# Attention with alternating local and full heads, and turned outputs in the local scores' bank

## What is computed

```python
# A: 8 local heads (2 key heads), a window of 128 keys to each side, a bias by distance, a sink per head
s = einsum(q, k_window) * scale + bias;  s = where(valid, s, -1e30)
m = max(max(s), sink);  e = exp(s - m);  p = e / (sum(e) + exp(sink - m));  oa = p @ v_window
# B: 8 full heads (2 key heads), over all T keys
p = softmax(einsum(q, k) * scale);  ob = p @ v
mixed = concat([rmsnorm(oa, g_out_a), rmsnorm(ob, g_out_b)])
```

## Time and profile before

| | us |
|---|---|
| median of 3 runs | 1623.55 (1623.14 to 1625.81) |
| the profiled execution | 1623.36 |
| its span | 1621.5 |
| TensorE busy | 1447.0 (89%) |
| VectorE busy | 932.7 (58%) |
| ScalarE busy | 721.8 (45%) |
| GpSimd busy | 182.2 (11%) |
| mean granted TensorE clock | 0.947 |

### The profile page before, as it was taken

How to read it: one execution, slowest core, us unless ns; L and a number is a source line. 1 busy time by engine, 2 the same in 40 slices (tenths; PEclk the granted TensorE clock), 3 DMA queues, 4 the chain that set the end, 5 groups by cost and what they waited for, 6 DMA issues and landing times. The chain is left out here.

```text
span 1621.5 us, 21520 instructions
## 1 busy us (share of the span) xinstructions
PE 1447.0 (89%) x7320; PEld 1016.2 (63%) x7320; DVE 932.7 (58%) x1324; ACT 721.8 (45%) x1157; POOL 182.2 (11%) x255
## 2 busy tenths in 40 slices
PE   5999997599999969869998969999999999948997
PEld 4777775365565535458887746666666666627885
DVE  5444443377677748723347856677676676643553
ACT  4333433376666747722221544444444444423332
POOL 1111111000000000010000111112112121021110
PEclk9999998699999979989998979999999999978999
DMA  8533322713111054064432756878878788753331
GB/s 257 94 111 110 110 97 85 252 64 114 70 63 55 20 190 156 29 208 156 140 123 87 262 169 220 263 252 270 256 261 267 254 262 265 245 164 126 126 135 65
DMA packets 118847, 261.53 MB, mean 161 GB/s; under 512 B 7648, under 2 KB 37472, under 8 KB 115720
## 3 DMA queue, kind: packets, MB, share of 16 engines
q1 hardware_dynamic: 110592, 233.55, 41.2%
q0 software_dynamic: 7168, 25.17, 6.7%
q10 hardware_dynamic: 1032, 2.10, 1.1%
HBM read 194.20 MB, written 66.58 MB: 161 GB/s over the span
## 5 line engine op out<-in xcount | busy, mean ns | idle before, releaser
L1742 DVE TENSOR_TENSOR moe_w_lo<-ring,moe_w_hi 128x2048 fp32r<-128x2048 f32 x96 | 220.3, 2296 | 163.5 <-ACT moe_w_hi L1681 163.4
L1681 ACT ACTIVATE moe_w_hi<-ring 128x2048 fp32r<-128x2048 f32 x96 | 183.7, 1914 | 204.0 <-PE moe_p_g L1864 82.2
L1413 PE MATMUL mix_p_big<-kept_out_w,mix_m_hi 128*128 128x512 f32 x384 | 126.4, 411 | 4.6 <-DVE mix_m_lo L1288 2.4
L510 PE MATMUL proj_p_out<-proj_w_hi,proj_h_hi 128*128 128x512 f32 x264 | 110.8, 420 | 9.5 <-DVE proj_q_hl L408 9.5
L1872 PE MATMUL moe_p_gu<-ring,moe_xT_r 128*64 128x512 f32 x512 | 116.9, 598 | 0.0
L510 PE MATMUL proj_p_out<-proj_w_lo,proj_h_hi 128*128 128x512 f32 x264 | 105.0, 398 | 0.0
L510 PE MATMUL proj_p_out<-proj_w_hi,proj_h_lo 128*128 128x512 f32 x264 | 104.9, 397 | 0.0
L962 DVE TENSOR_REDUCE sample_ntop<-sample_p_s 128x1 f32<-128x1024 f32 x64 | 78.2, 1222 | 37.4 <-PE sample_p_s L784 36.7
L798 PEld LDWEIGHTS sample_p_t<-sample_ident_r,sample_probs_r 128*128 128x128 f32 x688 | 73.1, 142 | 23.2 <-ACT sample_probs L900 6.6
L1413 PEld LDWEIGHTS mix_p_big<-kept_out_w,mix_m_hi 128*128 128x128 f32 x384 | 73.1, 196 | 21.4 <-issue 2.6
L798 PE MATMUL sample_p_t<-sample_ident_r,sample_probs_r 128*128 128x128 f32 x688 | 80.1, 246 | 5.0 <-ACT sample_probs L900 2.5
(11 more groups left out here) (298 smaller groups left out, 3122.4 us busy)
## 6 DMA issues: line engine op xcount, KB each, us to landing
ring<-in_w_gate SPq DMA_DIRECT2D x32, 1024.0 KB, 5.6
ring<-in_w_up SPq DMA_DIRECT2D x32, 1024.0 KB, 7.6
ring<-in_w_down SPq DMA_DIRECT2D x32, 1024.0 KB, 7.2
qT_d<-proj_qT SPq DMA_DIRECT2D x12, 1024.0 KB, 3.9
sample_q<-qT_d SPq DMA_DIRECT2D x8, 1024.0 KB, 5.3
proj_x<-in_x SPq DMA_DIRECT2D x12, 512.0 KB, 4.3
proj_w_raw<-in_w_in SPq DMA_DIRECT2D x8, 768.0 KB, 5.6
kT_d<-proj_kT SPq DMA_DIRECT2D x12, 512.0 KB, 3.6
```

Source lines behind the costliest of these rows:

```text
L510: last = pe.matmul(p_out[:, cols], h[:, s, k, :], w[:, k, cols], start=(k == 0 and n == 0), stop=(k == KC - 1 and n == 2))
L1413: mm = pe.matmul(p_out[:, cols], m[:, s, k, :], ww[:, k, cols], start=(k == 0 and n == 0), stop=(k == KC - 1 and n == 2))
L1681: act.activation(w_hi[:, at % SPLIT], raw[:, at % RAW], ACT.Copy).then_inc(hi_made, 1)
L1742: dve.tensor_tensor(w_lo[:, at % SPLIT], raw[:, at % RAW], w_hi[:, at % SPLIT].bitcast(F32), ALU.subtract).then_inc(lo_made, 1)
```

## The change

`attend` is rewritten; nothing else but the load of bias and sinks. The loops over tiles go, and all tiles are written out.

- The order of heads is alternating: local 0, full 0, local 1, full 1 and so on. In a run's first tile it is four local heads first, then pairs, then the last four full heads.
- A head is turned three steps after its scores (`LAG`), not two.
- Local scores have one bank, `p_sa`; full scores two slots of their own (`p_sb`, four banks for T = 1,024). The turned outputs go into `p_sa`, so `p_ot` goes; in the drain the last full output uses `p_sb`.
- A local head's maximum, negated and with the sink taken in, comes from one instruction: scores and bias are stored negated in `s_a`, and ScalarE's exponential has scale -1.
- `pT_b` is doubled. Local values are made in one group in step 2 of the next tile, the full ones over the next tile, in steps 5, 8, 11 and 14 (for four tiles: 6 and 11). With the local ones these are five groups.
- The turned local output is made in step 7 of the next tile, the full one in step 3 of the tile after that; the drain has all that is left.
- Queries are loaded in halves (local heads, then local keys, then full heads), values later; bias and sinks are issued by ScalarE. The splitting of weights is spread over steps 8 and 12 of all four tiles of the second run.

```diff
-    def load(self, sp):
-        sp.dma_start(self.bias[:], self.rel_d[:, :, P - 1:P - 1 + SPAN]).then_inc(self.landed, 16)
-        sp.dma_start(self.sinks[:], self.sink.partition_broadcast(P)).then_inc(self.landed, 16)
+    def load(self, act):
+        act.dma_start(self.sinks[:], self.sink.partition_broadcast(P)).then_inc(self.landed, 16)
+        act.dma_start(self.bias[:], self.rel_d[:, :, P - 1:P - 1 + SPAN]).then_inc(self.landed, 16)
...
+    LAG = 3
+    even = [h // 2 + (h % 2) * HEADS for h in range(STEPS)]
+    early = [0, 1, 2, 3, 8, 4, 9, 5, 10, 6, 11, 7, 12, 13, 14, 15]
+    order = [(u, head) for u in range(n) for head in (early if u == 0 else even)]
+    PV_B = {5: (0, 2), 8: (2, 4), 11: (4, 6), 14: (6, 8)} if n == 8 else {6: (0, 2), 11: (2, 4)}
...
-        p_s = a.ps("p_s", [P, 2, 2 * BANK])
+        p_sa = a.ps("p_sa", [P, BANK])
+        p_sb = a.ps("p_sb", [P, 2, max(T, BANK)])
...
# TensorE: waits of the scores (the rest of scores and turn is as before)
+                if head < HEADS:
+                    if g != at_a[0]:
+                        pe.wait_ge(ntop_done, at_a[at_a.index(g) - 1] + 1)
+                    for group in (A, B):
+                        if turned_before(g)[group]:
+                            pe.wait_ge(o_made[group], turned_before(g)[group])
...
+                    b = at_b.index(g)
+                    if b >= 2:
+                        pe.wait_ge(exp_done, at_b[b - 2] + 1)
...
+            def values_a(u):
+                for bank in range(2):
+                    pe.wait_ge(t_out[bank], evicted(bank, last_of(u, A) + 1))
+                pe.wait_ge(va_landed[u % 2], u // 2 * 16 + 16)
+                if u:
+                    pe.wait_ge(oT_out[B], u)
+                values(u, A, *edges(u))
...
+            def turn_o(u, g, step):
+                pe.wait_ge(oT_out[g], u + 1)
+                pe.wait_ge(ntop_done, min(step, END))
...
+            for g in range(END):
+                u, j = divmod(g, STEPS)
+                if j == 3 and u >= 2:
+                    turn_o(u - 2, B, g)
+                if j == 7 and u >= 1:
+                    turn_o(u - 1, A, g)
+                scores(g)
+                if u >= 1 and j == 2:
+                    values_a(u - 1)
+                if u >= 1 and j in PV_B:
+                    values_b(u - 1, *PV_B[j])
+                if g >= LAG:
+                    turn(g - LAG)
+            turn(END - 3)
+            turn_o(n - 2, B, END)
+            turn(END - 2)
+            values_a(n - 1)
+            turn(END - 1)
+            values_b(n - 1, 0, n // 2)
+            pe.wait_ge(o_made[B], n - 1)
+            turn_o(n - 1, A, END)
+            values_b(n - 1, n // 2, n)
+            turn_o(n - 1, B, END)
...
# ScalarE
+            for g in range(END + LAG):
+                u, j = divmod(g, STEPS)
+                if g >= LAG:
+                    copy_turned(act, 0, g - LAG, copy)
+                if g < END:
+                    exponentials(g)
+                    if next_chunk(u, j) is not None:
+                        w.high(act, next_chunk(u, j))
+                if 1 <= u < n:
+                    if j == 1:
+                        sink(u - 1)
+                    if j == 3:
+                        out_of_psum(u - 1, A)
+                    if j == 4 and u >= 2:
+                        square(u - 2, B)
+                    if j == 8:
+                        square(u - 1, A)
+                    if j == 15:
+                        out_of_psum(u - 1, B)
...
# VectorE
-                    dve.tensor_tensor_reduce(s_a[:, head % 2, lo * P:hi * P], p_s[:, head % 2, lo * P:hi * P],
-                                             bias[:, head, lo * P:hi * P], 1.0, -3e38, ALU.add, ALU.max,
-                                             top[:, head:head + 1]).then_inc(scored, 1)
-                    dve.scalar_tensor_tensor(out=ntop[:, s, head:head + 1], in0=top[:, head:head + 1], scalar=-1.0,
...
+                    dve.tensor_tensor_reduce(s_a[:, i % 2, cols], p_sa[:, cols], bias[:, head, cols], -1.0,
+                                             nsinks[:, head:head + 1], ALU.add, ALU.min, top).then_inc(ntop_done, 1)
...
+            for g in range(END):
+                u, j = divmod(g, STEPS)
+                if j == 3 and u >= 2:
+                    rows(u - 2, B)
+                if j == 7 and u >= 1:
+                    rows(u - 1, A)
+                maximum(g)
+                if j and next_chunk(u, j - 1) is not None:
+                    w.low(dve, next_chunk(u, j - 1))
+                if g >= LAG:
+                    copy_turned(dve, 1, g - LAG, copy)
...
+            copy_turned(dve, 1, END - 3, copy)
+            rows(n - 2, B)
+            copy_turned(dve, 1, END - 2, copy)
```

More of the change, by code:

```diff
@@ L646, in attend, with p_out, p_turned, turned_before @@
         block = ctx.enter_context(nc.Block())
[L648 to L680, removed]
+        def p_out(u, g):
+            return p_o[:] if u < n - 1 or g == A else p_sb[:, 0, 0:BANK].rearrange("p (h q) -> p h q", h=GROUP)
+        def p_turned(u, g):
+            bank = p_sa[:] if u < n - 1 or g == A else p_sb[:, 1, 0:BANK]
+            return bank.rearrange("p (h q) -> p h q", h=GROUP)
+        def turned_before(g):
+            u, j = divmod(g, STEPS)
+            return (max(0, u - (j <= 7)), max(0, u - 1 - (j <= 3)))
+        def next_chunk(u, j):
+            return 2 * u + (8, 12).index(j) if w and j in (8, 12) else None
         @block.sync
@@ L787, in turn @@
-            def turn(i, head, fresh, first, last):
-                pe.wait_ge(exp_done, i * 16 + head + 1)
-                lo, hi = edges(first, last) if head < HEADS else (0, 4)
-                for r in range(rounds(head)):
-                    bank = round_of(0, head, r) % 2
-                    if not (fresh and round_of(0, head, r) < 2):
-                        pe.wait_ge(t_out[bank], half(i) + round_of(0, head, r) // 2)
+                    pe.wait_ge(qa_landed[s], u // 2 * 32 + 32)
+                if head == HEADS:
+                    pe.wait_ge(qb_landed[s], u // 2 * 16 + 16)
+                    if u == 0:
+                        pe.wait_ge(kb_landed, 16)
@@ new lines, in scores, with turn @@
+                for cols in spans:
+                    for part in range(2):
+                        made = pe.matmul(out[:, cols], q_sb[:, s, head, :], keys[:, 2 * kv + part, cols],
+                                         start=(part == 0), stop=(part == 1))
+                made.then_inc(qk_done, 1)
+            def turn(g):
+                u, head = order[g]
+                lo, hi = edges(u) if head < HEADS else (0, 4)
+                pe.wait_ge(exp_done, g + 1)
+                for r in range(rounds[g]):
+                    m = first_round[g] + r
+                    if m >= 2:
+                        pe.wait_ge(t_out[m % 2], m // 2)
@@ L858, in _ @@
-            pe.wait_ge(ident_ready, 1)
-            run(pe, tile)
-            for head in (14, 15):
-                turn(n - 1, head, False, False, True)
-            for j in range(3, HEADS):
-                values_b(n - 1, j)
-            turn_o_b(n - 1)
-        def copy_turned(eng, bank, i, s, head, first, last, fresh, copy):
-            kv, g = head % HEADS // GROUP, head % GROUP
-            for r in range(rounds(head)):
-                n_round = round_of(0, head, r)
-                if n_round % 2 != bank:
+            pe.wait_ge(ident_ready, 1)
@@ new lines, in _, with copy_turned @@
+            turn_o(n - 2, B, END)
[7 more added lines that the diff above has]
+            turn_o(n - 1, B, END)
+        def copy_turned(eng, bank, g, copy):
+            u, head = order[g]
+            lo, hi = edges(u)
+            kv, h = head % HEADS // GROUP, head % GROUP
+            for r in range(rounds[g]):
+                m = first_round[g] + r
+                if m % 2 != bank:
```

441 lines of the change are left out of this document (196 added, 245 removed).

## The result

| | before | after |
|---|---|---|
| median, 4 runs each | 1624.68 us (1623.14 to 1626.76) | 1641.76 us (1638.20 to 1642.11) |
| profiled execution, span | 1623.36, 1621.5 | 1641.98, 1640.2 |
| TensorE, VectorE, ScalarE busy | 1447.0, 932.7, 721.8 | 1444.0, 921.6, 713.9 |
| mean granted clock | 0.947 | 0.939 |

The kernel after takes 1.0095 times as long, 95% interval 1.0079 to 1.0111. The prediction was 1628 (1612 to 1637): slower, as it said, but 14 us further. All three engines are busy for less time than before, so what came is idle time, part of it with a lower clock.

The account below looks back on a forecast made before the run. TensorE was taken to bound the first run (about 3 us of waits per 33.85 us tile), VectorE the second's inner tiles. First run +2.4 and second +2.1 on 1623.36 us gave 1627.9, so 1628 us, range 1612 to 1637.

Parts of the forecast that it names:

- Inner tiles: First run, tiles 1 to 6: -1.8 us, 33.7 a tile; TensorE waits 1.0, 0.8, 0.9 in steps 2, 5, 10.
- Rival A: Inner-tile waits are covered, half of each in the walk: 1613 us, an inner tile under 32.5 us; chance 0.22.
- Bias: First run's start: bias through ScalarE's queue lands 0.5 us later; start to tile 1 -0.4 us (bounds -4 and +4).
- The late end: Worst case for the first run's bias: it lands 3 us later, behind an equal number of larger rows.
- The sign named for this part: First run's start: prediction is wrong if its scores start before 302 us or after 306 us.
- First run's last tile and drain: Tile 7 to its last scores 31.5 us (+0.8); the drain +3.8 us (bounds +1 and +7).
- the term for the clock: First run's drain: 1.3 us added for a lowered clock, as in the drain before, with more gaps now.
- Second run's drain: By the same steps as the first run's drain: 11.8 us against 6.82, +5.0 us.
- Second run's tiles: Start -1.2 us; VectorE ends inner tiles; tile 1 24.0, tile 2 25.0, tile 3 21.7 us to last scores: -1.7.
- The negation "worth nothing in the first run": Removing the local heads' separate negation alone: nothing in the first run, up to 0.1 us per head in the second.
- B: The clock falls in the second run's three tiles (+3 each) and longer in both drains (+2): 1639 us; chance 0.18.
- C: A draw: drains cost only +1 and +3, the start gives its 2 us: 1622 to 1625 us; chance 0.18.

Follow-up runs that it names:

- e7: The kernel after, with ScalarE emptying the product bank in step 3 ahead of that step's copy and exponentials: 1636.38 us, 1.0056 of before.
- e6: The kernel after, with first-run turned local probabilities all copied by ScalarE, full heads' rounds by ScalarE then VectorE: 1639.49 us, 1.0087 of before.
- e8: The kernel before with only the separate negation taken away (fused into the local maximum's instruction): 1620.30 us, 0.9966 of before.
- e1: The kernel after, with bias and sinks issued by SyncE again, behind the first tile's local queries and keys: 1636.73 us, 1.0059 of before.
- e3: The kernel after, with SyncE's later loads held back until ScalarE's bias and sinks have landed: 1637.56 us, 1.0062 of before.
- e4: The kernel after, with weight splitting as before, in the second run's first and last tiles: 1640.98 us, 1.0088 of before.
- e13: The kernel after, with unread products in the second run's start and drain and more at its tile edges: 1636.58 us, 1.0076 of before.
- e9: The kernel after, with products that nothing reads in the second run's start and drain waits: 1638.46 us, 1.0081 of before.
- e2: The kernel before with one edit, bias and sinks issued by ScalarE: 1628.59 us, 1.0017 of before.
- e10: The kernel after with bias on SyncE's queue, a rearranged last tile with short drain, and the product bank emptied first: 1622.95 us, 0.9981 of before.
- e14: First run as in e10, second run as in the kernel before with the negation fused (e8): 1617.59 us, 0.9949 of before.

## Why the prediction was right and wrong

Term by term, in the profiled executions, as differences to before in us:

| | predicted | measured |
|---|---|---|
| first run, start to tile 1 | -0.4 | +5.4 |
| tiles 1 to 6 | -1.8 | -2.7 |
| tile 7 | +0.8 | +1.7 |
| drain | +3.8 | +4.0 |
| second run, start to tile 1 | -1.2 | +0.6 |
| tiles 1 to 3 | -1.7 | -0.8 |
| drain | +5.0 | +10.2 |
| sum | +4.5 | +18.4 |

- **Inner tiles: right.** 200.45 us for tiles 1 to 6 (201.3 predicted), a tile of 33.63 (33.7), waits of 0.79, 0.70 and 0.85 us (1.0, 0.8 and 0.9) at the places named. e7 shows the second as a price of its own. e6 shows that the other two are not: taken from VectorE they come back at ScalarE. Rival A falls. But of the 2.7 us that tiles 1 to 6 won, 1.6 are what the negation alone wins in the old order (201.55 in e8 for 203.12).
- **Bias: the step that failed first.** "+0.5, at worst 3 us later": it was +6.6, and 5.4 at the start of tile 1 (-0.4 predicted, at most +4). The late end took an equal number of rows on both queues. They did go one for one from 300 to 310 us, but SyncE's queue was ahead before that (735 packets to 335 by 300 us) and went faster again behind it: up to the first maximum it moved 1868 packets, 4.78 MB, to ScalarE's 1184, 1.58 MB. 18.77 us at 338 GB/s are 6.3 MB, where before it was 12.18 at 300, 3.7 MB: some 2.7 MB more stood ahead of the first maximum, and at 338 GB/s that is 8.0 us; the higher rate gives 1.4 of them back. The edit that was meant to take the bias out of a queue put it behind more. The sign named for this part (first scores before 302 or after 306 us) was written for the wrong instruction: the first scores stood at 297.76 us before, and 303.05 was VectorE's start, which came at 312.18.
- **First run's last tile and drain: right within 1 us**, 32.40 (31.5) and 17.8 (17.6). The drain is no fixed price, though. In after, e1, e3, e4 and e13 the same code took 18.8 to 18.9 us from the start of the last scores, at a clock of 0.91; in e9 it took 2.3 us more, at 0.76. So the term for the clock, 1.3 us, is met in part by luck.
- **Second run's drain: right mechanism, wrong size.** 16.97 for 11.8. Filled it is 13.2: 3.8 us were the clock's, and by 1.4 the walk was short at the full clock; which waits these are is not shown. The prediction gave the first drain 1.3 us for the clock and this one, with longer waits for its work, nothing. That was the second step that failed.
- **Second run's tiles.** Tile 2 25.04 (25.0), limited by VectorE as said, with some 0.6 us of it the clock's (e13). Tile 1 23.17 (24.0). Tile 3 23.43 (21.7): at a full clock it is 21.6, so the term was right for a clock that it didn't have. Start and tile 0 together 27.2 (25.4): half the queries let the scores start 0.6 us earlier, not 2, and TensorE waited 1.83 us for a copy of ScalarE's that stood behind the first chunk of weights; in e4, without that chunk, tile 0 took 1.7 us less.
- **The negation "worth nothing in the first run"**: 0.3 us a tile (e8). In the sum it was in the walk, so it moved no number there, but it is the one part of the change that these runs show as a gain by itself.
- **Rivals.** B's mechanism came, in the second run only, with its sign (a clock of 0.85 in tile 3 to the start of its last scores) and in fewer places than B had: 1.8 us in tile 3 and 3.8 in the drain. With the bias it carries the time past B's 1639. C and A didn't come. The range ended at 1637 because it left out half of B and had no case for the bias.
- **Not explained:** the attention starts 2.5 us later than before. In 18 profiles with the same code ahead of it the start lies between 289.4 and 295.8 us, the latest in e2; so one profile against one can't put these 2.5 us down to the change; nor the 2.2 us less behind the attention.
- In the prediction's first paragraph, eight listed instructions of full values are two blocks, not four; the 1.87 us and the sum are not touched.

## What to carry to other kernels

Before a load goes to a second queue, count the packets of both queues, not the bytes: while both are full it gets every other packet, and with small rows beside large ones it lands late. A drain's price is its waits and its clock: where a few waits near 1 us come just before products, write the sum at both clock levels. An order that wins where TensorE sets the tile can lose in a shorter run of the same code; price the runs apart, and choose for each.

## What the runs showed of the hardware

- Two queues that were both full shared packet for packet: 590 and 589 in 8 us (4 KB rows beside 1.5 KB ones), 753 and 740 in 6 (rows of some 1.5 KB on average in both).
- Products that nothing reads, put into waits of 0.5 to 1.7 us, held the granted clock of a 13.2 us drain at 1.00, which was 0.70 without them. The Trainium skill (TensorE: Matmul & The Clock Gate, section HAM oscillation) tells of waits for loads that lower the clock again and again; here waits on ScalarE and VectorE did.
- The same code in the same place met different clocks: from the start of the last scores, the first run's drain took 18.8 us at 0.91 in the kernel after and 21.1 at 0.76 in e9; in e10 and e14, alike there, 16.0 at 1.00 and 17.7 at 0.90; the second run's drain 17.5 at 0.71 in the kernel after and 16.0 at 0.79 in e1, whose edit is in the first run's loads alone. Some 2 us of a drain differ from one execution or kernel to the next with no cause that these runs show.
